# TensorE products of a chunked RWKV-7 scan: 64x64 tiles merged into 64x128 and 128x128 ones, and values transposed two chunks at a time

## What is computed

```
def rwkv7_mixer(h, shift_prev, s0, mu, w_r, w_k, w_v, w_o, w0, w1, w2, a0, a1, a2, g1, g2, k_k, k_a, r_k, ln_w, ln_b):
...
    kk = heads(k * k_k)
    kk = kk / jnp.maximum(jnp.sqrt(jnp.sum(kk * kk, axis=-1, keepdims=True)), 1e-12)
    k = k * (1.0 + (a - 1.0) * k_a)
...
    def step(s, inp):
        r_t, w_t, k_t, v_t, aa_t, bb_t = inp
        sa = jnp.einsum('bhij,bhj->bhi', s, aa_t)
        s = s * w_t[:, :, None, :] + sa[..., None] * bb_t[:, :, None, :] + v_t[..., None] * k_t[:, :, None, :]
        return s, jnp.einsum('bhij,bhj->bhi', s, r_t)
    s_last, ys = lax.scan(step, s0.astype(f32),
                          (tm(r_h), tm(w_h), tm(k_h), tm(v_h), tm(-kk), tm(kk * a_h)))
    y = tm(ys)
    mean = jnp.mean(y, axis=-1, keepdims=True)
    var = jnp.mean(jnp.square(y - mean), axis=-1, keepdims=True)
    yn = ((y - mean) * lax.rsqrt(var + GN_EPS)).reshape(bsz, t, c) * ln_w.astype(f32) + ln_b.astype(f32)
    bonus = (jnp.sum(r_h * k_h * r_k.astype(f32), axis=-1, keepdims=True) * v_h).reshape(bsz, t, c)
    out = ((yn + bonus).astype(h.dtype) * g) @ w_o
```

## Time and profile before

| | us |
|---|---|
| time, median of 3 runs | 3143.02 (3140.69 to 3143.58) |
| span of the profiled execution | 3144.1 |
| of it before the scan's first product | 1652 |
| scan, 1652 to 2136 | 484 |
| after the scan | 1008 |
| PE busy over the span | 3010.5 (96%) |
| DVE, ACT, POOL busy | 1805.6, 1023.8, 965.1 |

### The profile page before, as it was taken

One profiled execution on the slowest core, in us unless ns is written; L12 is line 12 of the kernel. 1 busy time (PEld: TensorE's weight loads), 2 busy tenths in 40 slices (PEclk: granted clock), 3 DMA queues, 4 the chain that ended last, 5 costly groups with the idle time before them and its releaser, 6 DMA issues.

```text
span 3144.1 us, 66739 instructions
## 1 busy us (share of the span) xinstructions
PE 3010.5 (96%) x29234; PEld 2891.6 (92%) x29234; DVE 1805.6 (57%) x1884; ACT 1023.8 (33%) x1281; POOL 965.1 (31%) x549
## 2 busy tenths in 40 slices
PE   8999999999999997889998999998999999999998
PEld 7899999999999997889997777887999999999997
DVE  7766765555656557512206777773566555565657
ACT  6533411111111113633326667764311111111113
POOL 1322223222222223313314555552132322222221
PEclk9999999999999999999998999999999999999999
DMA  3111111111111111242232222213111111111111
GB/s 107 46 44 41 39 44 41 48 48 41 48 41 48 41 48 34 81 174 86 90 110 73 70 69 71 75 48 102 41 48 41 41 48 48 41 48 41 48 41 71
DMA packets 88684, 185.66 MB, mean 59 GB/s; under 512 B 29024, under 2 KB 53088, under 8 KB 88416
## 3 DMA queue, kind: packets, MB, share of 16 engines
q1 hardware_dynamic: 81504, 154.73, 15.6%
q10 hardware_dynamic: 6912, 26.84, 2.1%
HBM read 145.01 MB, written 36.53 MB: 58 GB/s over the span
## 4 chain that ended last, share of the span: by engine, by line
PE 78%; DVE 14%; ACT 5%; issue 1%; POOL 1%; DMA 1%; DVEq 0%; SPq 0%; ACTq 0%; POOLq 0%
PE PS L1306 64%; PE PS L1516 10%; DVE T L1764 3%; DVE X L1764 2%; DVE T L1779 2%; PE PS L1442 2%; ACT T L512 2%; DVE BK L1764 1%; DVE HL L1774 1%; ACT L512 1%; DVE G L1764 1%; PE PS L1396 1%; DVE T L1774 1%; ACT UV L512 1%; PE PS L1358 1%
## 5 line engine op out<-in xcount | busy, mean ns | idle before, releaser
L1089 POOL TENSOR_TENSOR WL<-RAW,WH 128x1024 fp32r<-128x1024 f32 x204 | 496.0, 2432 | 1393.4 <-ACT WH L512 1389.5
L1306 PE MATMUL PS<-HH,WH 128*128 128x364 f32 x3456 | 771.8, 331 | 31.9 <-DVE HL L1774 12.7
L1306 PE MATMUL PS<-HH,WL 128*128 128x364 f32 x3456 | 767.4, 330 | 0.0
L1306 PE MATMUL PS<-HL,WH 128*128 128x364 f32 x3456 | 764.3, 330 | 0.0
L1306 PEld LDWEIGHTS PS<-HH,WH 128*128 128x128 f32 x3456 | 601.1, 189 | 41.5 <-issue 15.8
L1306 PEld LDWEIGHTS PS<-HH,WL 128*128 128x128 f32 x3456 | 605.7, 189 | 0.0
L1306 PEld LDWEIGHTS PS<-HL,WH 128*128 128x128 f32 x3456 | 603.0, 189 | 0.0
L512 ACT ACTIVATE WH<-RAW 128x1024 fp32r<-128x1024 f32 x204 | 216.7, 1062 | 825.9 <-PE PS L1306 809.6
L1764 DVE TENSOR_TENSOR T<-PS,T 128x1092 f32<-128x1092 f32 x110 | 142.6, 1296 | 552.4 <-PE PS L1306 535.6
L1764 DVE TENSOR_TENSOR X<-PS,X 128x1092 f32<-128x1092 f32 (+2 forms) x240 | 292.8, 1220 | 235.1 <-PE PS L1306 216.6
L1306 PE MATMUL PS<-PH,WH 128*128 128x364 f32 x1248 | 278.2, 331 | 10.2 <-DVE X L1764 5.2
(11 more groups left out here) (191 smaller groups left out, 3458.8 us busy)
## 6 DMA issues: line engine op xcount, KB each, us to landing
RAW<-weights SPq DMA_DIRECT2D x204, 512.0 KB, 3.3
scratch<-T ACTq DMA_DIRECT2D x31, 546.0 KB, 3.1
scratch<-SR ACTq DMA_DIRECT2D x14, 546.0 KB, 2.9
X<-xT SPq DMA_DIRECT2D x8, 546.0 KB, 7.7
T<-scratch_m SPq DMA_DIRECT2D x8, 512.0 KB, 3.7
KK<-scratch SPq DMA_DIRECT2D x16, 192.0 KB, 2.9
LW<-scratch SPq DMA_DIRECT2D x16, 192.0 KB, 2.8
AA<-scratch SPq DMA_DIRECT2D x16, 192.0 KB, 3.2
```

The costliest lines, as they stand in the source:

```text
L1089: pool.tensor_tensor(out, full, hi, ALU.subtract).then_inc(*t.made(event))
L1306: mm = pe.matmul(acc[:, j, :], a, b[:, j * CW:(j + 1) * CW], start=(i == 0 and q == 0), stop=(i == len(blocks) - 1 and q == 2))
```

## The change

1. **Head sums.** One product with the full 128x128 block-diagonal matrix of ones for both heads, where there were two 64x64 ones. The readers wait for one event in place of two.
2. **Products.** The two key blocks of a head, which lie side by side in `BK`, become one stationary operand of 128 columns: two products for each chunk where there were four, each 64 rows by 128 columns. The result in PSUM is the same.
3. **Values.** Two chunks (128 columns) are turned by one PE transposition, into bank 3 for head 0 and bank 4 for head 1. A batch of 5 chunks turns its fourth chunk twice (`two`). ACT now makes four copies to `UV` of 3 chunks each, or, for a batch of 5, four of 2 chunks and two of one chunk. `value_copies` counts them for the waits.

```diff
--- before.py
+++ after.py
+def two(a, z):
+
+    return [*range(a, z - 1, 2), *([z - 2] if (z - a) % 2 else [])]
+
+
+def value_copies(job):
+
+    return sum(4 + 2 * ((BATCHES[j % NB][1] - BATCHES[j % NB][0]) % 2) for j in range(job + 1))
...
                         act.wait_ge(*t.next("k_tv", 2))
+                        n = (pz - pa) // 2
                         for h in range(HEADS):
-                            run(UV[HALF[1 - h], pa:pz, h, :], bank(3, pz - pa, HALF[1 - h]), ACT.Copy, "k_vt", own=False)
+                            for s in range(2):
+                                run(UV[HALF[1 - h], pa + s:pa + 2 * n:2, h, :], bank(3 + h, n, HALF[s]), ACT.Copy, "k_vt", own=False)
+                            if (pz - pa) % 2:
+                                run(UV[HALF[1 - h], pz - 1, h, :], PS[HALF[1], 3 + h, n * CHUNK:(n + 1) * CHUNK], ACT.Copy, "k_vt", own=False)
...
-                    for h in range(HEADS):
-                        mul(PS[HALF[h], 2, 0:src.shape[-1]], CO[HALF[h], C_BD + h * CHUNK:C_BD + (h + 1) * CHUNK],
-                            src[HALF[h]], event)
+                    mul(PS[:, 2, 0:src.shape[-1]], CO[:, C_BD:C_BD + P], src, event)
...
                     for i in range(ga, gz):
-                        for s in range(2):
-                            for h in range(HEADS):
-                                mul(tile(3 + h, (h + s) % 2, i - ga, P), BK[HALF[h], i, s if h == 0 else 2 - s, :],
-                                    AR[HALF[h], i, :, :].rearrange("p s c -> p (s c)"), "k_g" if i == gz - 1 else None)
+                        for h in range(HEADS):
+                            mul(PS[:, 3 + h, (i - ga) * P:(i - ga + 1) * P], BK[HALF[h], i, h:h + 2, :].rearrange("p s c -> p (s c)"),
+                                AR[HALF[h], i, :, :].rearrange("p s c -> p (s c)"), "k_g" if i == gz - 1 else None)
...
-                    for i in range(pa, pz):
+                    for slot, i in enumerate(two(pa, pz)):
                         for h in range(HEADS):
-                            mul(tile(3, 1 - h, i - pa), VV[HALF[h], i * CHUNK:(i + 1) * CHUNK], IST[HALF[h], :],
-                                "k_tv" if i == pz - 1 else None)
+                            mm = pe.transpose(PS[:, 3 + h, slot * CHUNK:(slot + 1) * CHUNK],
+                                              VV[HALF[h], i * CHUNK:(i + 2) * CHUNK], IST[HALF[h], :])
+                            if i + 2 == pz:
+                                mm.then_inc(*t.made("k_tv"))
...
-                        dve.wait_ge(*t.next("k_g", 4))
+                        dve.wait_ge(*t.next("k_g", 2))
```

More of the change, by code:

```diff
@@ L448, in interval @@
                     f, b = divmod(job + 4, NB)
-                    sp.wait_ge(*t.at("k_g", 8 * (job + 2)))
+                    sp.wait_ge(*t.at("k_g", 4 * (job + 2)))
                     sp.wait_ge(*t.at("k_bonus", job + 2))
@@ L979, in values @@
                         act.wait_ge(*t.next("k_tv", 2))
+                        n = (pz - pa) // 2
                         for h in range(HEADS):
-                            run(UV[HALF[1 - h], pa:pz, h, :], bank(3, pz - pa, HALF[1 - h]), ACT.Copy, "k_vt", own=False)
+                            for s in range(2):
+                                run(UV[HALF[1 - h], pa + s:pa + 2 * n:2, h, :], bank(3 + h, n, HALF[s]), ACT.Copy, "k_vt", own=False)
+                            if (pz - pa) % 2:
+                                run(UV[HALF[1 - h], pz - 1, h, :], PS[HALF[1], 3 + h, n * CHUNK:(n + 1) * CHUNK], ACT.Copy, "k_vt", own=False)
                 def group_ln():
                     if has_n:
-                        act.wait_ge(*t.next("s_var", 2))
+                        act.wait_ge(*t.next("s_var"))
                         run(q1, PS[:, 2, 0:(nz - na) * CHUNK], ACT.Ln, "k_gln", scale=1.0 / CHUNK, bias=GN_EPS, own=False)
@@ L1476, in first_key_squares @@
                 pe.wait_ge(*t.at("k_sq", 1))
-                for h in range(HEADS):
-                    pe.matmul(PS[HALF[h], 2, 0:BW], CO[HALF[h], C_BD + h * CHUNK:C_BD + (h + 1) * CHUNK], X2[HALF[h], 0:BW],
-                              start=True, stop=True, skip_group_check=True).then_inc(*t.made("s_kk"))
+                pe.matmul(PS[:, 2, 0:BW], CO[:, C_BD:C_BD + P], X2[:, 0:BW],
+                          start=True, stop=True, skip_group_check=True).then_inc(*t.made("s_kk"))
             for j in range(3):
@@ L1668, in products @@
                     if g == 0:
-                        held(("k_bk", q + 1), ("k_bkh", q + 1), ("k_bk1", q + 1), ("k_arr", q + 1), ("k_ar", q + 1), ("k_vt", 2 * q + 2),
+                        held(("k_bk", q + 1), ("k_bkh", q + 1), ("k_bk1", q + 1), ("k_arr", q + 1), ("k_ar", q + 1), ("k_vt", value_copies(q)),
                              *([("k_pp", job + 1)] if has_s else []))
@@ L1705, in lower_and_spread @@
                     if has_l:
-                        held(("k_mc", mc * (inv + 1)), ("k_vt", 2 * inv + 2))
+                        held(("k_mc", mc * (inv + 1)), ("k_vt", value_copies(inv)))
                     for i in range(6):
@@ L2148, in floor @@
                     if has_k:
-                        dve.wait_ge(*t.next("s_kk", 2))
+                        dve.wait_ge(*t.next("s_kk"))
                         ts(X2[:, klo:khi], PS[:, 2, 0:khi - klo], 1e-24, None, ALU.max, ALU.bypass, "k_max", own=False)
@@ L2187, in bonus @@
                     if has_p:
-                        dve.wait_ge(*t.next("s_bon", 2))
+                        dve.wait_ge(*t.next("s_bon"))
                         if q == 0:
@@ L2233, in centred @@
                     if has_n:
-                        dve.wait_ge(*t.next("s_mean", 2))
+                        dve.wait_ge(*t.next("s_mean"))
                         stt(flat(Y)[:, ncols], PS[:, 2, 0:(nz - na) * CHUNK], -1.0 / CHUNK, flat(Y)[:, ncols],
```

## The result

The changed kernel takes 3152.7 us (median of 6 runs, 3149.4 to 3154.3), the kernel before 3142.6 (6 runs, 3139.0 to 3144.3): a ratio of 1.0031, 95% interval 1.002 to 1.0043. The forecast was 3155, range 3146 to 3173. The profiled execution of the changed kernel has a span of 3151.0 us, 6.9 more than the 3144.1 in the earlier trace rows; the medians lie 10.2 apart. A span is not a time: in every run the device time is 1.8 to 1.9 us above the span. The profiled execution after has 3152.85 us and so lies at its median. That of before comes to about 3146 (an estimate, 3144.1 + 1.85), above all six of its timed runs and 3.4 above their median (the 1.1 given ahead of the prediction sets a span beside a time). That is where the two differences part.

What follows compares the result with a forecast made beforehand. One chain through PE, ACT and DVE was taken to bound the scan, with PE busy 3010.5 of 3144.1 us. Switches +12.9, ACT copies +1.5, fewer records -2, first_key_squares -0.3 made +12.1 us: 3155, range 3146 to 3173.

Steps and rivals of the forecast that it cites:

- The small term ahead of the scan: Ahead of the scan, first_key_squares no longer changes tile shape between projections: -0.3 us.
- The price of a switch: On PE, each change of tile shape between steps costs 0.14 us, 0.09 of it at the border; 12 new an interval.
- rival 3: In products, the row halves don't run together, so products cost twice, 30 us more: 3185; chance 0.05.
- means: Head sum ahead of powers: two new switches, 0.28 us, partly covered by DVE's work; 0.20 us an interval left.
- variances: Head sum behind solved: one new switch, 0.14 us, covered by the 0.56 us wait ahead of grow(2); 0.
- key_squares: Head sum ahead of left_times(3): two switches, 0.28 us, 0.13 left after cover, none without link(0); mean 0.09 us.
- `products` and `bonus_sums`: Steps products(0), bonus_sums, products(1): five new switches, 0.70 us, partly covered ahead of DVE's masks; 0.27 us an interval left.
- `values`, PE and ACT: At value_turn, PE's 0.4 us saving hides behind state(1); ACT's copies cost 0.2 us in each 5-chunk batch, +1.5 us.
- Fewer records: In the scan, 992 of 14102 PE records fewer, 7%, end a third of the issue gaps: -2 us, bounds 0 and -6.
- Nearly nothing is covered: Across the scan, each late PE step makes DVE and ACT late too, which hand it on: 3164 to 3174; chance 0.12.
- The drains fall into waits that exist: On PE in the scan, the switches only fill waits already there: 3141 to 3149; chance 0.09.
- The supply of instructions is the real limit: Fewer PE records end most mid-step gaps, and earlier ACT copies help, if path switches stay under 0.2 us: 3133; chance 0.06.

Runs made afterwards that it cites:

- m_means: The kernel before with the head sum of means alone merged to one 128x128 product: 3147.4 us, ratio 1.0014.
- e5_sums_products: The kernel before with head sums and products merged, values left as before: 3149.9 us, ratio 1.0027.
- e3_values: The kernel before with only the values turned two chunks at a time by transposition, with the changed ACT copies: 3141.9 us, ratio 0.9999.
- e4_split: The kernel before with each head sum cut into four pieces of columns, same 64x64 tiles, 1140 records more: 3154.7 us, ratio 1.0039.
- m_var: The kernel before with the head sum of variances alone merged: 3143.0 us, ratio 1.0002.
- m_bonus: The kernel before with the head sum of bonus_sums alone merged: 3141.9 us, ratio 1.0004.
- e6_products_values: The kernel before with products merged and values turned by transposition, head sums left as before: 3142.4 us, ratio 0.9997.
- e2_products: The kernel before with the two products steps alone merged, two products for each chunk: 3141.0 us, ratio 0.9998.
- e8_products_var: The kernel before with products and the head sum of variances merged, the rest as before: 3141.4 us, ratio 1.0000.
- e7_after_split: The changed kernel with each head sum cut into four pieces of columns, same shapes: 3174.6 us, ratio 1.011 on the kernel before.

## Why the prediction was right

**Bound and place.** Right. Only the scan changed, and each part costs by where it stands. The small term ahead of the scan came as well: `first_key_squares` and the three records behind it take 1.14 us to the next step, where they took 1.40, and the border in front of it is gone (0.08): 0.3 us, as forecast.

**The price of a switch.** Right where it shows: 0.85, 0.84 and 0.74 us for `Y,CO`, `Q,CO` and `X,CO`, forecast 0.65 + 0.09 on the way out and the same again on the way in. Counted from the start of `key_turn`, `powers` starts 0.29 to 0.30 us later in `m_means` than before, in all three kinds of interval; two switches were to cost 0.28. The check for rival 3, 0.87 against 1.7 us, came out at 0.89 (1.09 less 0.20), with the halves together. The Trainium skill's rule that a change of tiling mode drains TensorE ("TensorEngine Tiling (Array Packing)", Key Properties) agrees with `m_means`, where the records fall, the streaming stays, and the kernel is slower.

**What lies on the path**, in us an interval:

| term | forecast | alone | together |
|---|---|---|---|
| `means` | 0.20 | 0.16 | |
| `variances` | 0 | -0.03 | |
| `key_squares` | 0.09 | 0.15 | |
| `products` and `bonus_sums` | 0.27 | 0.11 + 0.02 | 0.18 + 0.02 |
| `values`, PE and ACT | 0.065 (1.5 us in 23) | 0.13 | 0.11 |
| sum | 0.63 | | 0.63 |

The total agrees to 0.04, the terms don't, and that is luck: `key_squares` and `values` cost 0.10 more together than forecast, `means`, `products` and `bonus_sums` about as much less. `key_squares` was mis-sized: I counted 0.13 in the intervals with `link(0)`, and they show 0.16 and 0.25. `products` and `bonus_sums` have more cover than I gave them: the head sum there stands in front of `products(1)`, which waits for DVE's `masked(0)` anyway, so the 0.02. Part of that cover is gone once the sums ahead are late as well, as `e5_sums_products` shows. The remaining 0.04, between 0.30 for the four and 0.34 for all sums, I can't place; differences of 0.03 lie within the spread of such intervals.

**Values.** The PE side came as told: `link(2)` still starts 0.06 us behind `state(1)`. From the last transposition to `link(2)` it is 0.20 us in the interval shown above and 0.25 to 0.33 in `e3_values`, part of it waiting. The ACT side I under-counted. I had the 16 batches of 6 at nothing, since `value_turn` ends 0.38 us earlier for copies 0.34 longer. But `value_turn` itself starts 0.16 us later in `e3_values` (0.24 in one kind of interval), behind its own new border, and `products(0)` waits for the copies (1.3 us in 6 waits in its trace). Counted from the start of `value_turn`, the last copy of a batch of 6 ends after 1.84 us in place of 1.94, so 0.06 of the 0.16 are left; that of a batch of 5 after 1.85 in place of 1.71, less 0.12 that there was to spare, so 0.18 are left. For batches of 5 the six copies took 1.38 us, less than the 1.57 of my sum, since two of them overlap the copy ahead by 0.10 each.

**Fewer records.** The term that was mis-sized, first in its count. I had 992 records fewer, 7%; the traces have 1136, 8%, because a transposition is one record where the product that it replaces was two. And I took -2 us for them, a third of the gaps, with bounds 0 to -6. In the profiled pair the stalls above the undisturbed interval fell by 7.4, and the visible gaps from 5.1 to 0.3 in 400 us. The supply of instructions comes in packets of a fixed count, and with fewer records PE needs them less often: 0.234 packets of queue 8 in a us of the scan before, 0.211 in the changed kernel, 0.244 in `e4_split`. That the gaps hang on these packets is shown above; at which pace they begin to come too late is not.

**Sum against the medians.** The +14.5 and -7.4 belong to the profiled pair, and of that pair the execution of before is some 3.4 us above its median, while the one after is at it. So of the 7.4 about 3 us are the luck of one execution: 14.5 less the 10.2 between the medians leaves about 4 us (5 with 0.67 for 0.63) for the stalls that the fewer records usually save. That is an estimate, since no run shows the stalls of a usual execution of before, but the gaps of the four kernels with 48 records fewer (1.5 to 4.1 us where before had 5.1) point the same way. Twice the forecast's 2 us, it accounts for the 2 us by which the change, +10.2, stayed under the forecast +12.1; 2 to 3 us is also what these comparisons resolve.

**The rivals.** "Nearly nothing is covered" falls with `m_var` and `m_bonus`. "The drains fall into waits that exist" holds for these two alone. "The supply of instructions is the real limit" had the right mechanism, and `e4_split` and `e6_products_values` show it at work, but its condition (under 0.2 us an interval on the path) fails in the changed kernel at 0.63. Where the condition holds, in `e2_products`, `e3_values`, `e6_products_values` and `e8_products_var` (0.11, 0.13, 0.18, 0.12), the result is a draw, not a gain.

## What to carry to other kernels

Before merging small TensorE products into one of another tile shape, count the borders that it makes in the order of the steps, price one from two neighbouring steps of the trace, and ask of each whether a wait stands behind it. A shape that differs from both neighbours pays twice. By these prices a merge could win only where neighbours of the same shape come with it or the count of records is what binds; no run here shows such a win. Where PE's trace has "issue" gaps in mid-step, look at how many records lie between them: here their number cost time like any other resource.

## What the runs showed of the hardware

- Gaps without a releaser on PE come at distances that are multiples of about 126 matmul records (with 126 weight loads), and 98 of 101 end 1.2 to 1.65 us after a 16384-byte packet of the instruction queue q8 has landed: PE waits for its instructions. They depend on how dense the records are: 5.1 us in 400 with 14102 records in the scan, 0.3 with eight per cent fewer, 14.5 with eight per cent more. Each figure is one execution, and with 48 records fewer than before four kernels had 1.5 to 4.1.
- The eight 128x128 fp32 records of 96 columns in `e7_after_split` follow each other at 0.11 us, and the head sum takes 1.06 us to the next step, where the pair of 64x64 tiles with the same 96 columns takes 0.083 and the uncut sum takes 0.84. The weight loads of these records (PEld) fill the whole stretch and follow each other at the same 0.11 us. That they set the pace would fit; no run separates it.

```profile
1852.23 0.97 PEld L1529 LDWEIGHTS PS<-Q,CO 128*128 128x128 f32 x8
```

- ACT's copies from one half of PSUM's partitions and then the other follow each other without overlap: four of 192 columns 1.37 us, two of 384 1.00. Cutting a copy in two so costs ACT some 0.18 us. In a batch of 5 the single chunk comes from the same half as the copy ahead of it and starts 0.10 us before that one ends.
